# A weight stream of 1 MiB entries: two more expert entries held beside the ring and sent ahead of block 1's attention

## What is computed

```python
def hier_moe(h, ...):                      # 32 experts in 4 groups of 8, top 2, D_FF = 256
    g_prob = softmax(t @ w_group_router + b_group_router)
    g_w, g_idx = top_k(g_prob, 1)
    e_logits = (t @ w_expert_router + b_expert_router)[group g_idx]
    e_w, e_idx = top_k(softmax(e_logits), 2)
    combine = ...                          # g_w * e_w / sum(e_w), one row of 32 per token
    a = einsum('nd,edf->nef', t, w_gate)
    b = einsum('nd,edf->nef', t, w_up)
    routed = einsum('nef,efd->nd', silu(a) * b * combine, w_down)
    shared = (silu(t @ w_sh_gate) * (t @ w_sh_up)) @ w_sh_down
    return routed + shared

def reference(...):
    x = first_block(...)     # mixer, then hier_moe, each with a residual and norms
    return second_block(x, ...)
```

## Time and profile before

| | |
|---|---|
| device time, median of 3 runs | 697.21 us |
| the three runs | 698.68, 697.21, 695.96 us |
| span of the profiled execution, first to last instruction | 693.2 us |
| what lies around the span, by the median | 4.0 us |
| TensorE matmuls busy (PE) | 643.9 us, 93% |
| weight loads into TensorE busy (PEld) | 482.9 us, 70% |
| VectorE (DVE), ScalarE (ACT), GpSimd (POOL) busy | 351.3, 290.2, 51.7 us |
| read from HBM | 179.04 MB, 260 GB/s over the span |
| mean granted TensorE clock | 0.972 of full |

### The profile page before, as it was taken

One profiled execution on the slowest core, in us unless ns is written; L12 is line 12 of the kernel. 1 busy time (PEld: TensorE's weight loads), 2 busy tenths in 40 slices (PEclk: granted clock), 3 DMA queues, 4 the chain that ended last, 5 costly groups with the idle time before them and its releaser, 6 DMA issues.

```text
span 693.2 us, 10210 instructions
## 1 busy us (share of the span) xinstructions
PE 643.9 (93%) x4037; PEld 482.9 (70%) x4037; DVE 351.3 (51%) x678; ACT 290.2 (42%) x552; POOL 51.7 (7%) x75
## 2 busy tenths in 40 slices
PE   8999899999997876779899999999999999999996
PEld 5979788832542421233379999989788888888884
DVE  4687664731130120110086766557866666666665
ACT  5855572421010110100083645473665555554454
POOL 3100101100010000000048100000000000000001
PEclk9999999999998987888999999999999999999999
DMA  8926308999999999999997343335545555555101
GB/s 344 419 73 257 122 1 347 426 408 425 427 418 421 422 419 421 423 421 422 419 420 306 121 155 140 122 125 187 186 172 182 182 188 185 205 202 191 61 1 61
DMA packets 26286, 180.73 MB, mean 261 GB/s; under 512 B 3184, under 2 KB 3312, under 8 KB 5120
## 3 DMA queue, kind: packets, MB, share of 16 engines
q1 hardware_dynamic: 25488, 177.89, 64.9%
q10 hardware_dynamic: 752, 2.21, 0.8%
HBM read 179.04 MB, written 1.05 MB: 260 GB/s over the span
## 4 chain that ended last, share of the span: by engine, by line
PE 72%; DMA 15%; DVE 6%; ACT 4%; issue 2%; SPq 0%; POOLq 0%; POOL 0%; ACTq 0%; DVEq 0%
PE ps L1532 69%; DMA ring<-stream_dram 15%; PE ps L1535 3%; DVE ring_r L384 1%; ACT single L377 1%; DVE work L1467 1%; DMA vec<-small_dram 1%; ACT work L815 1%; DVE work L1470 1%; DVE h L1520 0%; ACT turned L820 0%; ACT work_r L811 0%; DVE work L1353 0%; ACT work L722 0%; ACT turned_w L731 0%
## 5 line engine op out<-in xcount | busy, mean ns | idle before, releaser
L1532 PE MATMUL ps<-turned,single 128*128 128x256 f32 (+2 forms) x944 | 231.3, 326 | 1.6 <-ACT work L592 0.8
L1532 PE MATMUL ps<-turned,ring_r 128*128 128x256 f32 (+1 forms) x648 | 179.8, 281 | 0.0
L1532 PEld LDWEIGHTS ps<-turned,single 128*128 128x128 f32 x944 | 156.2, 189 | 18.5 <-issue 2.0
L384 DVE TENSOR_TENSOR ring_r<-ring,single 128x1024 fp32r<-128x1024 f32 (+1 forms) x132 | 160.8, 1241 | 14.8 <-ACT single L377 14.7
L377 ACT ACTIVATE single<-ring 128x1024 fp32r<-128x1024 f32 (+1 forms) x132 | 133.9, 1047 | 0.0
L1532 PEld LDWEIGHTS ps<-turned,ring_r 128*128 128x128 f32 x648 | 121.1, 188 | 0.4
L1532 PE MATMUL ps<-ring,work 128*32 128x512 f32 (+2 forms) x470 | 72.1, 623 | 18.1 <-DMA ring<-stream_dram 16.3
L1532 PE MATMUL ps<-work 128*128 128x128 f32 (+5 forms) x318 | 60.9, 381 | 3.1 <-DVE work L1011 1.8
L1532 PEld LDWEIGHTS ps<-single 128*128 128x128 f32 x257 | 38.8, 191 | 34.5 <-issue 21.1
L1532 PE MATMUL ps<-single,turned 128*128 128x512 f32 (+3 forms) x208 | 59.7, 367 | 1.9 <-DVE turned L1152 1.6
L1532 PE MATMUL ps<-single 128*128 128x512 f32 (+1 forms) x257 | 56.1, 357 | 3.3 <-DVE single L1364 2.3
(11 more groups left out here) (248 smaller groups left out, 726.7 us busy)
## 6 DMA issues: line engine op xcount, KB each, us to landing
ring<-stream_dram SPq DMA_DIRECT2D x148, 1024.0 KB, 12.5
work<-stream_dram SPq DMA_DIRECT2D x12, 1024.0 KB, 13.4
turned_w<-stream_dram SPq DMA_DIRECT2D x4, 1024.0 KB, 15.0
ring<-stream_dram SPq DMA_DIRECT2D x2, 832.0 KB, 7.3
h<-x_dram SPq DMA_DIRECT2D x2, 512.0 KB, 4.5
gain<-gains_dram ACTq DMA_DIRECT2D x2, 512.0 KB, 8.3
yields<-stream_dram SPq DMA_DIRECT2D x1, 1024.0 KB, 15.2
out_dram<-work SPq DMA_DIRECT2D x4, 256.0 KB, 2.0
```

What stands on the lines that cost most here:

```text
L384: dve.tensor_tensor(ring_r[:, place, a], ring[:, place, a], w_hi[k % HIGHS][:, a].bitcast(F32), ALU.subtract).then_inc(s["wlo_done"], 1)
L1532: return pe.matmul(o, lhsT, rhs, start=start, stop=stop, **kw)
```

## The change

The room that the program reserves in SBUF for descriptors of dynamic DMAs goes from its default to 1 KiB per partition. A new tensor `extra` holds two entries. `ASIDE` goes from 9 to 11: entries 31 and 32 are now set aside too, in `extra`, with two semaphores `extra_full0` and `extra_full1`. Their loads stand in SP's list behind entry 10 and ahead of entry 11, without a wait of their own. As two entries fewer go through the ring at that place, all later ring entries sit two places further on: the eight ring entries behind the set-aside ones are now 33 to 40 (31 to 38 before), the eight that reuse set-aside rooms 41 to 48 (39 to 46 before), and the rest of the first two groups starts at 49. The order of loads of all other entries is as before. `route_c` and `route_d` are merged into `route_a` and `route_b`, whose second counts the engines now wait for.

```diff
-ASIDE, ASIDE_WORK = 9, 6
+ASIDE, ASIDE_WORK, EXTRA = 11, 6, 2
...
+        extra = sb("extra", [P, EXTRA, SLOT])
...
+        extra_full = [sem(f"extra_full{i}") for i in range(EXTRA)]
...
+            if i >= ASIDE - 1 - EXTRA:
+                return extra[:, i - (ASIDE - 1 - EXTRA), :]
...
+            elif ASIDE_END - EXTRA <= n < ASIDE_END:
+                eng.wait_ge(extra_full[n - (ASIDE_END - EXTRA)], 16)
...
-            order = list(range(2, MOE_AT + 6)) + list(aside[1:6]) + [MOE_AT + 6, MOE_AT + 7, *aside[6:8], aside[0], aside[8]]
+            order = list(range(2, 11)) + list(aside[9:]) + list(range(11, MOE_AT + 6)) + list(aside[1:6])
+            order += [MOE_AT + 6, MOE_AT + 7, *aside[6:8], aside[0], aside[8]]
...
+                    if n in aside[9:]:
+                        sp.dma_start(home(n), stream[entry_at(n)]).then_inc(extra_full[n - aside[9]], 16)
+                        continue
...
-            act.wait_ge(s["route_c"], 1)
-            act.activation(route[:, 12, 0:NT], route[:, 12, 0:NT], ACT.Exp).then_inc(s["route_d"], 1)
+            act.wait_ge(s["route_a"], 2)
+            act.activation(route[:, 12, 0:NT], route[:, 12, 0:NT], ACT.Exp).then_inc(s["route_b"], 1)
...
-            dve.tensor_tensor(rt_(12, 1), m2, m1, ALU.subtract).then_inc(s["route_c"], 1)
+            dve.tensor_tensor(rt_(12, 1), m2, m1, ALU.subtract).then_inc(s["route_a"], 1)
...
-                dve.wait_ge(s["route_d"], 1)
+                dve.wait_ge(s["route_b"], 2)
...
-    nc = bacc.Bacc("TRN2", target_bir_lowering=False, num_devices=1)
+    nc = bacc.Bacc("TRN2", target_bir_lowering=False, num_devices=1, dynamic_dma_scratch_size=1024)
```

More of the change, by code:

```diff
@@ L303, in two_blocks @@
             qt_ps qt_act qt_dve s_ps pad_done cu_done nm_done e_done p_done pt_ps pt_sb o_ps sq_done ssm_ps msm_done
-            rsm_done mix_ps mix_done h1_done xh_done xl_done hst_ps hst_sb lg_ps route_a route_b route_c route_d
+            rsm_done mix_ps mix_done h1_done xh_done xl_done hst_ps hst_sb lg_ps route_a route_b
             chosen_done rank_ps rounds_done sgu_ps ssg_done hs_done cms_done gmix_done gmoe_done dve_step pool_step sin_in tab_done
```

## The result

| | before | after |
|---|---|---|
| device time, median of 4 runs | 696.59 us | 692.69 us |
| lowest and highest | 695.88, 698.68 | 692.20, 693.87 |
| ratio, 95% interval | | 0.995 [0.9934, 0.9965] |
| span of the profiled execution | 693.2 us | 690.4 us |
| last expert entry landed | 346.0 us | 341.8 us |

The ratio is a gain of 3.5 us, with an interval from 2.4 to 4.6. The profiled execution of the change took 692.20 us, 1.8 us more than its span.

The account below looks back on a forecast made before the run. The weight stream was taken to set the end of the experts' stage, TensorE what follows. Two entries fewer (-4.98 us) and a possible tear (+0.2) gave -4.8: from 697.2 to 692.4 us, range 690.6 to 695.2.

Parts of the forecast that it names:

- The size of a load and of the gap: Full stretch of the weight stream, from 107.67 us: two entries fewer at 2.49 us each, -4.98 us.
- The place where the stream could tear: Ring load issued at 196.6 us: its successor waits for entry 49 and lands later, +0.2 us, between 0 and 2.6.
- TensorE meets the stream: Experts' stage: TensorE catches up at about entry 59 or 60 and passes on the full 4.8 us.
- the first rival: End of experts' stage: TensorE takes over early, gain cut to 2.3 to 3.8 us; chance 0.10.
- the same pattern of waits shortly before: Argument against TensorE taking over before the end of the experts' stage; no size of its own.
- The median from the span: Whole kernel: median of the runs taken as 4.0 us above the profiled span, 697.21 against 693.2 us.
- the bound of 0.5%: Whole kernel: smallest difference told from no change, 3.5 us, so faster means under 693.7 us.
- rival 2: Weight loads of the loop wait for slots, not bandwidth: no gain, 697.2 us; chance 0.07.
- rival 3: Queued weight loads' descriptors need the scratch: 4.8 instead of 2.49 us per load, about 911 us; chance 0.03.
- The rate: Full stretch: 1 MiB at the trace's 421 GB/s is 2.49 us; at about 358 GB/s 2.93, giving 691.5 us.

Follow-up runs that it names:

- the fourth of the change: The changed kernel measured again beside its three filler variants on one chip, no edit against the change: 692.34 us, ratio 0.9949 to the kernel before.

## Why the prediction was right, and where it was off

**The size of a load and of the gap.** -4.98 us for two loads held: the full stretch of the first profile is 4.80 us shorter. By the time, one load gave 2.2 us, two gave 3.5 to 3.8 over three measurements, and the same two loads issued at 106 us gave 0.6 us, not told from none. The last landing, averaged over the nine profiles with the change's order up to there, is 342.5 us; over the four with the order of before (with the run of the late extra loads) 346.8. That is 4.3 us, against 4.8 predicted.

**The place where the stream could tear.** The price of +0.2 us was right in the mean: the load that waits for entry 49 lands 0, 0.6, 1.1, 0, 0.3, 0, 0, 0.1 and 0 us beyond the stream's pace in the nine profiles, 0.2 on average. The largest was 1.1, where it was issued at 200.2 us instead of 198.8; the forecast had 199.9. The missing 0.5 us of the landing lies in single late loads elsewhere; whether the change makes more of them or these profiles had more by chance isn't settled.

**TensorE meets the stream, and from 336 us on does "the same work as before, started 4.8 us earlier".** This is the step that failed, and it is the first rival, to which I gave 0.10. Its mechanism was named rightly (TensorE is hardly faster than the stream there, and the low stretch may fall otherwise), its price of 1 to 2.5 us too (1.5), but in three of four profiles of the change it happened, in none of the four with before's landing times by more than 0.3 us. In the first profile TensorE had met the stream (its last wait for a load is at 331.84 us) and lost the time behind that; in the other two it waits for no load after 314 us. I took "the same pattern of waits shortly before" as a reason against it. That the low stretch ends some microseconds later relative to the stream is enough: in the first profile of before it was over 2.9 us ahead of the landing of the last half group's first entry, in the fourth of the change it ended 3.4 us behind it, and TensorE regains only 1.5 us over the entries left. On average it takes 1.1 us off the gain: 4.3 - 1.1 = 3.2, against 3.5 measured.

Whether the change itself makes the low stretch come later isn't shown. Up to the first fillers, near 313 us, all nine profiles with its order run the same program, and in only two of them had a stretch begun by then that reaches into the last half group; with before's order it is one of four, by 0.7 us.

**The median from the span.** I put 4.0 us between the span and the median. The execution with the 690.4 us span took 692.20, so 1.8 us lie around it, and another of before with 694.8 took 696.63. By the same 1.8 us the profiled execution of before took about 695.0 us (an estimate), less than each of the three runs that I took the median from. The later medians of before were 695.6 to 696.6, below the 697.21 I started from. So 692.4 was hit by two errors that nearly cancel: a start 0.6 us too high, and a gain that is 0.9 too large by the medians and 1.3 by the ratio. That the forecast is only 0.3 us off is luck to that extent. On the scale of the bound of 0.5% the gain lies at the bound, not clearly beyond it, and 0.76 for faster was too sure.

**Slots (rival 2).** Excluded by the run with the extra loads at 106 us and by the one extra entry.

**The scratch (rival 3).** Excluded: 1.0003 [0.9993, 1.0012] with the scratch and the semaphores alone. What the Trainium skill says in SBUF — State Buffer, "SBUF size: 192, 224, or 256?" (the 16 KiB serve the software path) agrees with that.

**The rate.** The Trainium skill, DMA: Bandwidth & Descriptors, "Specifications", gives about 358 GB/s per core, as half of what a stack of memory delivers. As a limit for this program, which runs on one core, that isn't borne out: 421 GB/s over 234 us, in the kernel after as in the one before.

## What to carry to other kernels

Where a stream of loads sets the pace of a stage, look for the moments when its queue is empty because the next load waits for room, and price extra room by the loads that fit in such a gap, not by its size. Follow the gain to where the consumer takes it up: an engine that catches up by 0.36 us per load, as here, can be late for the rest of the stage after one slow stretch. Fillers that keep the clock up are work on the path whenever the engine is behind, so measure them again after each change of the stream, and try none.

## What was not expected of the hardware

Single loads land 0.9 to 1.7 us behind the stream's 2.49 us pace, one to three of them between 108 and 342 us in each profile. One is seen in the timeline of the version without fillers above, where TensorE is idle for 2.97 us ahead of 327.61 instead of some 1.4. They explain much of the scatter of the last landing between profiles of one kernel (341.8 to 343.5 us).

The places are not arbitrary. Of the 14 profiles 13 have such a load at 119 to 122 us, and others recur near 148, 159, 183 and 216 us. The page of the kernel before lists another kind of packet (packets, MB, share of 16 engines):

```profile
q8 instruction: 32, 0.52, 0.3%
```

In each trace ten of these, of 16 KiB and 0.9 to 1.1 us each, fall into the full stretch. Of the 33 late loads in the 14 profiles 27 land 2.1 to 4.0 us behind the start of such a packet, though only one landing in eight lies between 1.5 and 4.5 us behind one. Of the other six, one is the load that waits for entry 49, and five land at about 148 us. But 113 of the 140 packets are followed by no late load, and no run moved them: that they delay the loads is likely, and not shown.

At half the granted clock the matmuls of an entry take 1.93 us instead of 1.06 and four fillers 2.08 instead of 1.20. Three of the four profiles with before's landing times had such a stretch between 305 and 319 us without any cost: it ended 1.6 to 2.9 us before the first entry of the last half group landed, and TensorE waited for loads again later.
